# Three of twelve modulation slabs move from the attention stage to the start of the projection stage, in a two-block transformer kernel

## The reference, cut to what matters

```python
mod_lat = jax.nn.silu(c) @ w_mod + b_mod          # w_mod: 1024 x 6144
mod_ctx = jax.nn.silu(c_ctx) @ w_mod + b_mod
sh1, sc1, g1, sh2, sc2, g2 = [m[:, None, :] for m in jnp.split(mod_lat, 6, axis=-1)]
csh1, csc1, cg1, csh2, csc2, cg2 = jnp.split(mod_ctx, 6, axis=-1)
```

## Time and profile before

| | us |
|---|---|
| median of 3 runs | 2504.05 (2496.58 to 2514.23) |
| the profiled execution | 2508.15 |
| its span | 2506.4 |
| PE busy in the span | 2261.6 (90%) |
| DVE, ACT, POOL busy | 980.7, 1161.0, 1210.0 (39%, 46%, 48%) |
| mean granted PE clock | 0.953 |

### The profile page before, as it was taken

How to read it: one execution, slowest core, us unless ns; L and a number is a source line. 1 busy time by engine, 2 the same in 40 slices (tenths; PEclk the granted TensorE clock), 3 DMA queues, 4 the chain that set the end, 5 groups by cost and what they waited for, 6 DMA issues and landing times. The chain is left out here.

```text
span 2506.4 us, 42020 instructions
## 1 busy us (share of the span) xinstructions
PE 2261.6 (90%) x18012; PEld 2022.2 (81%) x18012; DVE 980.7 (39%) x1984; ACT 1161.0 (46%) x1650; POOL 1210.0 (48%) x308
## 2 busy tenths in 40 slices
PE   8998989898998999898989999798965778998998
PEld 7997865488998999785568999776754777998997
DVE  2321654334221220356242320257756776323540
ACT  5432632365432542543255543555865554534342
POOL 6773610073875877440053877332311002585784
PEclk9999998899999999999989999999988898999999
DMA  7553522242654655432333554422112103453552
GB/s 247 170 171 106 171 85 68 84 160 94 193 173 139 194 177 170 127 118 85 118 101 101 178 181 147 132 87 67 53 48 54 35 18 103 129 189 119 179 183 94
DMA packets 303655, 316.41 MB, mean 126 GB/s; under 512 B 7833, under 2 KB 295053, under 8 KB 303213
## 3 DMA queue, kind: packets, MB, share of 16 engines
q1 hardware_dynamic: 303469, 313.72, 39.2%
HBM read 311.53 MB, written 2.16 MB: 125 GB/s over the span
## 5 line engine op out<-in xcount | busy, mean ns | idle before, releaser
L368 POOL TENSOR_TENSOR slab_lo<-ring,slab_hi 128x2048 fp32r<-128x2048 f32 (+1 forms) x242 | 1091.7, 4525 | 794.7 <-ACT slab_hi L357 758.0
L357 ACT CAST slab_hi<-ring 128x2048 fp32r<-128x2048 f32 (+1 forms) x242 | 451.5, 1870 | 556.0 <-PE bank L438 265.4
L433 PE MATMUL bank<-ffn_h_hi,slab_hi 128*128 128x256 f32 x1344 | 331.2, 284 | 0.0
L434 PE MATMUL bank<-ffn_h_lo,slab_hi 128*128 128x256 f32 x1344 | 329.7, 283 | 0.0
L433 PEld LDWEIGHTS bank<-ffn_h_hi,slab_hi 128*128 128x128 f32 x1344 | 257.9, 192 | 0.5 <-issue 0.3
L434 PEld LDWEIGHTS bank<-ffn_h_lo,slab_hi 128*128 128x128 f32 x1344 | 258.0, 192 | 0.1
L400 PE MATMUL bank<-ffn_hidden_hi,slab_hi 128*128 128x256 f32 x704 | 199.3, 283 | 0.0
L401 PE MATMUL bank<-ffn_hidden_lo,slab_hi 128*128 128x256 f32 x704 | 199.2, 283 | 0.0
L402 PE MATMUL bank<-ffn_hidden_hi,slab_lo 128*128 128x256 f32 x704 | 199.2, 283 | 0.0
L438 PE MATMUL bank<-ffn_h_hi,slab_lo 128*128 128x256 f32 x1344 | 189.0, 283 | 4.4 <-POOL slab_lo L368 4.4
L438 PEld LDWEIGHTS bank<-ffn_h_hi,slab_lo 128*128 128x128 f32 x1344 | 173.3, 192 | 5.2 <-POOL slab_lo L368 5.2
(11 more groups left out here) (638 smaller groups left out, 5535.9 us busy)
## 6 DMA issues: line engine op xcount, KB each, us to landing
ring<-in_ffn_w_in SPq DMA_DIRECT2D x88, 1024.0 KB, 5.1
ring<-in_ffn_w_out SPq DMA_DIRECT2D x32, 1024.0 KB, 5.0
ring<-in_w_in SPq DMA_DIRECT2D x30, 1024.0 KB, 5.4
ring<-in_mix_w_in SPq DMA_DIRECT2D x24, 1024.0 KB, 5.3
ring<-in_w_mod SPq DMA_DIRECT2D x24, 1024.0 KB, 5.2
ring<-in_w_up SPq DMA_DIRECT2D x22, 1024.0 KB, 5.1
ring<-in_ffn_w_out SPq DMA_DIRECT2D x16, 768.0 KB, 4.3
ring<-in_mix_w_out SPq DMA_DIRECT2D x8, 1024.0 KB, 5.1
```

The source lines that it names most:

```text
L357: act.copy(self.hi[i % self.PLACES][:, 0:w], K.ring[n % RING][:, 0:w]).then_inc(self.hi_ready, 1)
L368: pool.tensor_tensor(self.lo[i % self.PLACES][:, 0:w], place[:, 0:w], self.hi[i % self.PLACES][:, 0:w].bitcast(F32), ALU.subtract).then_in ...
L433: pe.matmul(out, w[0][:, k, col], act[0][:, k, :], start=(k == 0), stop=False)
L434: pe.matmul(out, w[0][:, k, col], act[1][:, k, :], start=False, stop=False)
```

## The change

Modulation slabs 0 to 2 of each layer stand ahead of the projection's slabs in the ring's order. Slab 0 is multiplied at the start of the projection stage, ahead of PE's sums for the norm, and slabs 1 and 2 right behind these sums. ACT copies the three results to `zs` behind its part of the norm, PE turns them with six small transposes behind the first projection slab, and DVE copies them to a small new tile. The other nine are treated as before (three of them in `rwkv_stage`), with `AT_A_CALL` 1 in place of 2 and `AHEAD` 16 in place of 8: as many products ahead of the first attention step, and three in each step in place of six.

```diff
@@ layer_slabs
-    slabs += mix_slabs(K, mix, l)
-    slabs += [whole(K.a["w_mod_2"], l * (MOD_SLABS * HALF) + i * HALF) for i in range(MOD_SLABS)]
+    mod = [whole(K.a["w_mod_2"], l * (MOD_SLABS * HALF) + i * HALF) for i in range(MOD_SLABS)]
+    slabs += mod[0:MOD_FIRST] + mix_slabs(K, mix, l) + mod[MOD_FIRST:]
@@ project_stage, PE
+                def modulation(n):
+                    w = view(K.next_slab(pe))
+                    for k in range(KD):
+                        last = pe.matmul(K.bank[5 + n][0:2, 0:HALF], K.cs[:, k, :], w[:, k, :], start=(k == 0), stop=(k == KD - 1))
+                    K.slab_done(last)
+
+                modulation(0)
                 norm.pe(pe)
+                for n in range(1, MOD_FIRST):
+                    modulation(n)
                 pe.wait_ge(norm.h_ready, KD)
...
-                for n in range(0, 4):
+                project(0)
+                pe.wait_ge(mod_copied, MOD_FIRST)
+                for t in range(2 * MOD_FIRST):
+                    last = pe.transpose(K.bank[5][:, HALF + 2 * t:HALF + 2 * t + 2], zs[0:2, t // 2, (t % 2) * P:(t % 2 + 1) * P],
+                                        K.c("ident", slice(0, 2), n=2))
+                last.then_inc(turned, 1)
+                for n in range(1, 4):
                     project(n)
@@ project_stage, ACT and DVE
                 norm.act(act)
+                K.wait_slabs(act, n0)
+                for n in range(MOD_FIRST):
+                    act.copy(zs[0:2, n, :], K.bank[5 + n][0:2, 0:HALF]).then_inc(mod_copied, 1)
...
                 norm.dve(dve)
+                dve.wait_ge(turned, 1)
+                dve.tensor_copy(s["mod"][:, :, :], K.bank[5][:, HALF:HALF + 4 * MOD_FIRST].rearrange("p (t c) -> p t c", c=2))
@@ Modulations
-    AT_A_CALL = 2
+    COUNT = MOD_SLABS - MOD_FIRST
+    AT_A_CALL = 1
     FIRST = 3
-    AHEAD = 8
+    AHEAD = 16
@@ Modulations.pe_end
-        for t in range(2 * MOD_SLABS):
+        for t in range(2 * self.COUNT):
```

More of the change, by code:

```diff
@@ L35 @@
 MOD_SLABS = 12
+MOD_FIRST = 3
 LEVELS = (4, 5)
@@ L1119, in mixer @@
             s["es"] = K.sb("es", [P, 4, 4], ctx=rctx)
+            s["mod"] = K.sb("mod_begin", [P, 2 * MOD_FIRST, 2], ctx=rctx)
             project_stage(K, l)
@@ L1144, in project_stage @@
     nc, s = K.nc, K.mx
-    n0 = K.eaten
+    m0, n0 = K.eaten, K.eaten + MOD_FIRST
     n_slabs = len(MIX_ORDER)
@@ L1170, in project_stage @@
         bonus_in, bonus_summed, bonus_read = K.sem("bonus_in"), K.sem("bonus_summed"), K.sem("bonus_read")
-        turn_in, turned = K.sem("turn_in"), K.sem("turned")
+        turn_in, turned, mod_copied = K.sem("turn_in"), K.sem("turned"), K.sem("mod_copied")
         turn_banks = (4, 5, 2, 3, 6, 7)
@@ L1357, in _ @@
                 for i, dst in enumerate(("vtok_r", "vtok_r", "btok", "btok", "ktok", "ktok")):
-                    act.wait_ge(turned, i + 1)
+                    act.wait_ge(turned, i + 2)
                     act.copy(s[dst][:, i % 2, :], K.bank[turn_banks[i]][:, :])
@@ L1944 @@
 class Modulations:
-    AT_A_CALL = 2
+    COUNT = MOD_SLABS - MOD_FIRST
+    AT_A_CALL = 1
     BANKS = (6, 7)
     FIRST = 3
-    AHEAD = 8
+    AHEAD = 16
     def __init__(self, K, ctx):
         self.K, self.n0, self.k, self.n, self.copies = K, K.eaten, 0, 0, 0
-        self.rows = K.sb("mod_rows", [2, MOD_SLABS * HALF], ctx=ctx)
-        self.copied, self.turned, self.kept = K.sem("mod_copied"), K.sem("mod_turned"), K.sem("mod_kept")
+        self.rows = K.sb("mod_rows", [2, self.COUNT * HALF], ctx=ctx)
+        self.copied, self.turned = K.sem("mod_rows_copied"), K.sem("mod_turned")
     def first_place(self, n):
@@ L1982, in some @@
         for _ in range(self.AT_A_CALL):
-            if self.n == MOD_SLABS:
+            if self.n == self.COUNT:
                 return
@@ L1997, in act @@
         K = self.K
-        while self.copies < min(MOD_SLABS, self.FIRST + (self.AHEAD + step * calls) * self.AT_A_CALL // KD):
+        while self.copies < min(self.COUNT, self.FIRST + (self.AHEAD + step * calls) * self.AT_A_CALL // KD):
             n = self.copies
@@ L2006, in pe_end @@
         K = self.K
-        while self.n < MOD_SLABS:
+        while self.n < self.COUNT:
             self.some(pe)
-        pe.wait_ge(self.copied, MOD_SLABS)
-        for t in range(2 * MOD_SLABS):
+        pe.wait_ge(self.copied, self.COUNT)
+        for t in range(2 * self.COUNT):
             last = pe.transpose(K.bank[6][:, 2 * t:2 * t + 2], self.rows[:, t * P:(t + 1) * P], K.c("ident", slice(0, 2), n=2))
@@ L2014, in dve @@
     def dve(self, dve):
-        K, m = self.K, 2 * MOD_SLABS
-        dve.tensor_copy(K.mod[:, 0:m, :], K.mod[:, m:2 * m, :]).then_inc(self.kept, 1)
+        K, m, first = self.K, 2 * MOD_SLABS, 2 * MOD_FIRST
+        K.dve_own.after(dve, dve.tensor_copy(K.mod[:, 0:m, :], K.mod[:, m:2 * m, :]))
         dve.wait_ge(self.turned, 1)
-        dve.wait_ge(self.kept, 1)
-        dve.tensor_copy(K.mod[:, m:2 * m, :], K.bank[6][:, 0:2 * m].rearrange("p (t c) -> p t c", c=2))
+        dve.tensor_copy(K.mod[:, m:m + first, :], K.mx["mod"][:, :, :])
+        dve.tensor_copy(K.mod[:, m + first:2 * m, :], K.bank[6][:, 0:2 * (m - first)].rearrange("p (t c) -> p t c", c=2))
 class Attention:
@@ L2196, in _ @@
             def _(sync):
-                K.load_slabs(sync, mod.n0 + MOD_SLABS + RING)
+                K.load_slabs(sync, mod.n0 + mod.COUNT + RING)
             @block.tensor
@@ L2233, in _ @@
                 att.act(act, at_step=lambda i: (mod.act(act, i, att.CALLS), scan.act(act, i + EARLY - 1)))
-                mod.act(act, KD * MOD_SLABS, 1)
+                mod.act(act, KD * mod.COUNT, 1)
             @block.vector
```

## The result

The changed kernel takes 2490.57 us (median of 11 runs, 2485.2 to 2493.92), the kernel before beside it 2506.22 (11 runs, 2496.58 to 2514.23). The ratio is 0.9947, its 95% interval 0.993 to 0.9963: 13.3 us faster (9.3 to 17.5), which is within 1% of no change.

A forecast was written before the change was run, and what follows sets the result against it. PE bounds the kernel (busy in 90% of the span), without idle time in the attention steps but waiting in the projection stage. Attention -24.0, projection +3.7, clock +3 sum to -17.3 us: 2504.05 to 2487, range 2472 to 2503.

The forecast's parts named there:

- Steps up to the mean: Attention steps before the mean: 28 calls make one product in place of two, -12.4 us a layer.
- rival 3: Attention steps become bound by the softmax's chain and give back nothing: 2508 to 2514 us, chance 0.04.
- layer 1 in 49.6 us: Sign of being right: layer 1 from step 0's scores to the mean in 49.6 us (62.0 before), PE never idle.
- Mean to variance: Attention stage between mean and variance: four products now stand there and delay it, +1.1 us a layer (+0.4 to +2.0).
- End: End of the attention stage: 18 transposes in place of 24, -0.7 us a layer.
- Projection: Projection stage with 24 moved products a layer: +0.3 us in layer 0, +3.4 in layer 1, together +3.7 (+3 to +9.5).
- Rival 2: Projection stage pays in full, as the clock falls or products start later than ACT: +9.5 us, 2493 us, chance 0.12.
- Clock in the steps: Attention steps: thinner steps spend somewhat more time at half clock, +3 us in all, between nothing and 9.6.
- Rival 1: The clock stays up throughout, also in layer 0's first attention steps: 2474 to 2479 us, chance 0.15.
- Sum: Whole kernel: -24.0 + 3.7 + 3 = -17.3 us, median from 2504.05 to 2487 us.
- Rival 4: The clock stays at half through the attention steps: +46 us, 2550; in one layer alone 2522; chance 0.06.

The follow-up runs named there:

- the doubled products: The changed kernel with every modulation product of the attention steps made twice, the sixteen ahead of them once: 2503.94 us, ratio 1.0014 to the kernel before.
- the thinner kernels: The changed kernel with 17 or 20 modulation products in steps 0 to 9 in place of 28, twelve in the wait behind the variance: ratios 0.9981 and 0.9947.
- the second chip: The unchanged changed kernel timed again beside two follow-up kernels: 2489.55 us against 2500.06 for the kernel before, ratio 0.9959 (0.9937 to 0.998).

## Why the prediction held, point by point

- **Steps up to the mean, -12.4.** Taken as at full clock they went from 71.61 - 0.44 x 20.8 = 62.5 and 61.97 to 57.70 - 0.44 x 17.1 = 50.2 and 56.15 - 0.44 x 13.7 = 50.1: -12.1. The price was 0.432 a product, and a call of one 0.52 us (0.51 taken). PE never waits in them, so rival 3 falls. One sign that I had named for being right didn't come: layer 1 in 49.6 us. It took 56.15, since the clock was at half for 13.7 us of it; that belongs to the term of the clock below.
- **Mean to variance, +1.1.** It was +1.36, and 1.23 of it goes with the products: 6.25 us in the kernel without them. I had let ACT's slack swallow 0.2 us; it swallowed none.
- **End, -0.7.** -0.5 in layer 0.
- **Projection, +3.7.** +3.0: -0.1 and +3.0 for the +0.3 and +3.4. That layer 0 pays next to nothing rests on its longer half-clock stretch before (10.2 us), which other traces show in layer 1 or in neither; where it doesn't come, both layers pay some 3 us. Products at full clock from ACT's start, no gap, first cut slab at 246.02 (I had said 246.8, with the stage starting 0.42 us later). The kernel with three products there in place of 24 is only 2.0 us shorter, so the price is small because both waits and the clock are covered. Rival 2 falls.
- **Clock in the steps, +3.** In the profiled pair half-clock time went from 20.8 to 30.8 us, +4.4 us. But the term isn't as steady as I treated it: the second trace of before had 41.8 us, which would make it -5. That was an unusual execution (granted clock 0.948, median 0.953), so +4.4 is the better reading; still, +3 was a choice between nothing and 9.6, and that it came so near is in part luck. Of its reason as I put it, the doubled products and the thinner kernels show that the modulation products keep the clock up. That they do so by their 128 rows they don't show, and I had misread the steps: what they keep is not only products over 64 or 4 rows. I counted on steps 2 to 9 since they never fell, and in the changed kernel they didn't; with 17 or 20 products they did. Rival 1, a clock that stays up throughout, didn't come: the changed kernel's three traces all had 31 us at half in the two layers' steps.
- **Sum.** By traces -16.5 us in the places of the change, -17.3 forecast. The ratio of the runs makes it 13.3 (9.3 to 17.5), which holds both, and 10.3 (5.0 to 15.8) on the second chip. The spans of the profiled pair differ by 22.1, more than that: the profiled execution of before (2508.15) is 1.9 us above the median of the eleven runs beside the changed kernel, the profiled one of the changed kernel (2486.28) 4.3 below its own. I moved the anchor for an execution that stood 4.1 us above a median of three runs; with eleven it was 1.9, and 2506.2 - 17.3 is 2489 for a measured 2490.6. Whether the median execution of before has the slow stretch in one layer or in both isn't shown: the granted clock tells how much, not where.
- **Rival 4.** Chance 0.06, and it didn't come at three products a step. It was nearer than the profile of before let me see: at 17 products in ten steps it came. I had set it aside since those steps show no idle time, by the Trainium skill's rule (TensorE: Matmul & The Clock Gate, "A second HAM failure mode: psum-queue depth-cycling"), which looks to small idle times of the engine. Here a PE busy for 74.47 of 74.47 us was granted 0.54. The measurement decides: half the clock was granted here without any idle time.

## What to carry to other kernels

Work for PE that waits for nothing is worth most in PE's waits, and only as much of it as the wait is long: sixteen products in two waits of 1.85 and 5.68 us cost nothing, the eight beyond cost 3.1 us a layer. Thinning a stretch in which PE is always busy gives back less than the products' length when the clock falls for it: read the granted clock of that stretch before and after, and not only the busy time. And a stretch that runs at half in one layer and not in the other is a hint that a second trace of the kernel before is worth its price. Before a trace is taken to stand for its kernel, compare its granted clock with the median of the other runs.

## What was not expected of the hardware

- TensorE was granted half its clock for 69 of 74.5 us in which it was busy throughout. In these steps 164 of the 276 records beside the modulation products are over 64 or 4 rows (scores, parts of the scan), 112 over 128 rows; with 56, 40 or 41, and 28 modulation products among them (128 rows, a stationary side of 2 columns, each 0.43 us) the half-clock time was 0 to 21, 3 to 8, and 14 to 18 us. The Trainium skill says of one other kind of PE work that it doesn't lift the clock (TensorE: Matmul & The Clock Gate, "Part 4: PE-mode transpose"), which no run here shows. Whether in these steps it is the number of rows or another trait of the products isn't separated.
- The half-clock time of the steps repeats in the changed kernel (17 and 14 us, three traces), but which layer has which value changes from one execution to the next; in the kernel before 21 us of it in layer 1 came in one trace and not in the other.
- Raising the clock in a stretch in which PE mostly waits gave next to nothing: 10 us less at half behind the variance, 0.9 us gained. Over whole executions of the kernel before, where PE is busy for 90% of the span, a us at half cost 0.445 us (92 runs).
